# A hybrid attention layer on eight cores: the last tile's second MLP matmul by rows, and more filler held back where a buffer is waited for

## The reference

```python
proj = h @ w_in                       # 9728 columns: dilated q/k/v for 3 groups, q1,q2,k1,k2,v, two gates
y_a  = combine(dilated_attention(g) for g in 3 groups) @ w_proj_a     # windows of 128 keys, dilation 1, 4, 16
o_b  = (softmax(q1 k1) - lam * softmax(q2 k2)) @ v                    # causal over all 8192 keys, 8 heads
y_b  = (rms_norm(o_b) * (1 - lam_init)) @ w_proj_b
mix  = (sigmoid(gate_a) * y_a + sigmoid(gate_b) * y_b) @ w_out
h    = layer_norm(alpha * h + mix)
y    = layer_norm(alpha * h + square(relu(h @ w_mlp1)) @ w_mlp2)      # 1024 -> 4096 -> 1024
```

## Time and profile before

| | |
|---|---|
| runs | 4638.4, 4642.36 and 4921.69 us, median 4642.36 |
| the profiled execution | 4640.14 us; its span 4638.6 us, 1.5 us lie around it |
| slowest core / the other even cores | 4638.6 / 4621.7, 4619.8, 4614.2 us |
| odd cores | 4495.3 to 4510.2 us |
| PE busy on the slowest core | 4324.6 us, 93% |
| ACT, DVE, POOL busy | 2608.1, 1749.8, 854.4 us |

### The profile page before, as it was taken

How to read it: one execution, slowest core, us unless ns; L and a number is a source line. 1 busy time by engine, 2 the same in 40 slices (tenths; PEclk the granted TensorE clock), 3 DMA queues, 4 the chain that set the end, 5 groups by cost and what they waited for, 6 DMA issues and landing times.

```text
span 4638.6 us, 99445 instructions; the slowest of 8 cores (4495.3 to 4638.6 us)
## 1 busy us (share of the span) xinstructions
PE 4324.6 (93%) x37017; PEld 2471.5 (53%) x37400; DVE 1749.8 (38%) x3732; ACT 2608.1 (56%) x3329; POOL 854.4 (18%) x1113
## 2 busy tenths in 40 slices
PE   7898999799999899989988999999999999999998
PEld 3444454444455455445544655756657557566565
DVE  1655645412123322660033153242541533424353
ACT  1465655621166666677765566666665666767610
POOL 2000003311100011340013213022131130220322
PEclk9999999999999999999999999999999999999999
DMA  8665557877657866796476455474673664745363
GB/s 141 163 160 110 120 120 198 220 162 152 133 129 187 195 141 138 200 281 138 105 192 152 128 181 144 139 199 137 177 183 115 205 163 142 205 123 173 93 202 122
DMA packets 554463, 738.50 MB, mean 159 GB/s; under 512 B 165250, under 2 KB 352770, under 8 KB 552066
## 3 DMA queue, kind: packets, MB, share of 16 engines
q1 hardware_dynamic: 448450, 449.91, 35.7%
q0 software_dynamic: 105536, 282.11, 26.1%
HBM read 630.15 MB, written 191.87 MB: 177 GB/s over the span
## 4 chain that ended last, share of the span: by engine, by line
PE 79%; DVE 6%; DMA 5%; ACT 4%; issue 4%; SPq 2%; POOL 0%; DVEq 0%; ACTq 0%; POOLq 0%
PE PSB L639 48%; PE PSB L1388 19%; PE PSB L1360 11%; ACT m_PT_44 L425 1%; SPq L208 1%; DMA m_WR_147<-wp 1%; SPq L203 1%; DMA VA<-m_VAS_86 1%; DVE m_OO_50 L1431 1%; DVE m_TT_49 L1426 1%; DMA m_AK_97<-KA 1%; PE PSB L1489 1%; PE PSB L1523 1%; ACT m_PT_46 L425 1%; DVE m_TT_49 L1437 1%
## 5 line engine op out<-in xcount | busy, mean ns | idle before, releaser
L425 ACT ACTIVATE m_PT_43<-PSB 128x1024 bf16<-128x1024 f32 x544 | 556.8, 1023 | 577.1 <-PE PSB L1360 453.8
L425 ACT ACTIVATE m_PT_45<-PSB 128x1024 bf16<-128x1024 f32 (+1 forms) x544 | 530.2, 975 | 452.2 <-PE PSB L1360 371.4
L425 ACT ACTIVATE m_PT_44<-PSB 128x1024 bf16<-128x1024 f32 (+1 forms) x544 | 540.8, 994 | 0.1
L425 ACT ACTIVATE m_PT_46<-PSB 128x1024 bf16<-128x1024 f32 (+1 forms) x544 | 514.6, 946 | 2.1 <-DVE PSB L1372 1.7
L1372 DVE TENSOR_TENSOR PSB<-PSB,m_BT_72 128x512 f32<-128x512 f32 (+1 forms) x156 | 86.6, 590 | 196.5 <-PE PSB L1360 196.1
L1360 PE MATMUL PSB<-m_QB_69,m_KB_114 64*128 64x512 bf16 (+1 forms) x672 | 105.4, 378 | 31.3 <-DMA m_KB_114<-KTB 11.9
L1372 DVE TENSOR_TENSOR PSB<-PSB,m_BT_71 128x512 f32<-128x512 f32 (+1 forms) x156 | 86.2, 590 | 115.4 <-PE PSB L1360 115.3
L639 PE MATMUL PSB<-m_X1A,m_WR_146 128*128 128x512 bf16 x512 | 123.1, 379 | 1.7 <-ACT m_T_178 L425 1.0
L639 PE MATMUL PSB<-m_X1A,m_WR_149 128*128 128x512 bf16 x512 | 123.2, 379 | 1.3 <-DVE m_T_176 L1076 0.4
L639 PE MATMUL PSB<-m_X1A,m_WR_147 128*128 128x512 bf16 x512 | 122.4, 379 | 1.5 <-DVE m_T_178 L1076 1.0
L639 PE MATMUL PSB<-m_X1A,m_WR_148 128*128 128x512 bf16 x512 | 121.9, 379 | 1.3 <-ACT m_T_178 L425 0.9
(11 more groups left out here) (870 smaller groups left out, 10055.7 us busy)
## 6 DMA issues: line engine op xcount, KB each, us to landing
m_WR_146<-WB POOLq DMA_DIRECT2D x84, 512.0 KB, 6.3
m_WR_147<-WB POOLq DMA_DIRECT2D x84, 512.0 KB, 6.3
m_WR_148<-WB POOLq DMA_DIRECT2D x84, 512.0 KB, 6.0
m_WR_149<-WB POOLq DMA_DIRECT2D x84, 512.0 KB, 6.3
WB<-wm POOLq DMA_DIRECT2D x84, 256.0 KB, 20.4
m_VB_118<-VB SPq DMA_DIRECT2D x68, 258.0 KB, 4.8
m_VB_120<-VB SPq DMA_DIRECT2D x68, 258.0 KB, 4.6
m_KB_114<-KTB SPq DMA_DIRECT2D x68, 256.0 KB, 5.3
```

The source lines that it names most:

```text
L425: return self.P.op("scalar", lambda e: e.activation(out=out, in_=in_, func=func, bias=bias, scale=scale), 165.0 + 0.861 * n, rd, wr, gen)
```

## The change

The change has four parts.

1. In the last tile, `mlp2` runs block by block: the outer loop is s, the inner one q. The four W2 units of the quarters 2 and 3 have rooms of their own (`WZ`, which the order shows as `m_WZ_114` to `m_WZ_116` and `m_WZb_139`), laid over buffers of attention and gates that are no longer in use by then. They are loaded on POOL's queue at the start of the last tile's `mlp1`. The weight sequence of that tile ends with the four units of the quarters 0 and 1, which stay in the ring to the end.
2. The planner's estimate of when a DMA transpose has landed uses 130 bytes per ns in place of 300. Only the order follows from it; the DMA itself is the same.
3. `ensure` notes that it had to wait (`waited`), and `run` then fills for 8000 ns beyond the time of the unit's buffers, whether or not they are late; a first unit has no margin of its own any more, only the 1500 ns of any late unit.
4. `fill_until` may take 200 steps in place of 60.

```diff
-            done += slow / 60.0 + (nbytes - slow) / 300.0
+            done += slow / 60.0 + (nbytes - slow) / (130.0 if turn else 300.0)
...
-        self.soon = False
+        self.soon = self.waited = False
...
+        self.WZ = mk("WZ", [4096], BF16, 3, [a0])
...
+        self.WZ += mk("WZb", [4096], BF16, 1, [e2 - 8192])
...
-                w += [("m", M_W2 + i) for i in range(8)]
+                w += [("m", M_W2 + i) for i in range(4 if g[1] == self.tiles[-1] else 8)]
...
     def mlp1(self, t, wk):
...
+        if t == self.tiles[-1]:
+            for i, b in enumerate(self.WZ):
+                P.dma("gpsimd", b.ap, D["WB"][M_W2 + 4 + i], "g_" + b.name, 1 << 20, [self.dW[M_W2 + 4 + i]], gen=[b], split=2)
...
     def mlp2(self, t, wk):
...
+        rows = t == self.tiles[-1]
+        W = {}
+        for q, s in [(q, s) for s in range(4) for q in range(4)] if rows else [(q, s) for q in range(4) for s in range(4)]:
+            if q not in W:
+                W[q] = self.WZ[2 * q - 4:2 * q - 2] if rows and q > 1 else [self.weight(wk + 2 * q + i, "m", M_W2 + 2 * q + i) for i in range(2)]
...
+            if s == 3 and not rows:
+                self.release_w(2)
+                self.look_ahead(False)
...
         while L not in self.have:
+            self.waited = True
...
-        for _ in range(60):
+        for _ in range(200):
...
-            if t > P.T["tensor"]:
-                self.fill_until(t + (6000.0 if first else 1500.0))
+            self.fill_until(t + (8000.0 if self.waited else 1500.0 if t > P.T["tensor"] else 0.0))
+            self.waited = False
```

## The result

The changed kernel takes 4607.92 us (median of the first timing); the kernel before beside it 4642.36 us. The ratio is 0.9926, with a 95% interval from 0.9899 to 0.9952; timed a second time on another chip it was 0.9929 (0.9914 to 0.9945). For the sum of parts I use a second measure that scatters less than the slowest core, the mean span of the four even cores.

What follows compares the result with a forecast made beforehand. PE was taken as the bound, busy 4324.6 of 4638.6 us. From 4640.1, -7 - 3 - 9 + 1.5 + 0 - 5 + 0.3 + 1 = -21 gave 4619 profiled, median near 4620; whole range 4598 to 4646, the forecast's own 4610 to 4630.

Steps and rivals of the forecast that it cites:

- more is gained: Rival, chance 0.1: both O1 waits and the first wait go entirely, with their lost clock; -39 us, 4602.
- First unit: First QK matmul's 7.75 us wait for its K tile: 24 more filler matmuls fit in it; -7 us.
- Units held back: Wait of 4.20 us at 456.7 us: 12 more filler matmuls move ahead of it; -3 us.
- Filler dealt out differently: Between 400 and 2000 us: no wait seen to open or close; 0, with 8 us either way.
- Transposes: Second tile's O1: five bare units fill two waits, 19 us together, landing unchanged; -9 us.
- The bare units' bill: Units elsewhere that lose their filler: 0.3 to 0.5 us each where no wait covers it; +1.5 us.
- the waits move on: Rival, chance 0.2: at O1 the next K tile or the transpose comes later; total -8.5 us, 4632 to 4634.
- Last tile: Last tile by rows: -5 us behind PE's last matmul, +0.3 for a W2 wait, +1 for delayed W1 loading.
- slower: the new loads starve the ring: Rival, chance 0.1: in the last tile the fifth W1 unit lands late behind 4 MB; +4 us, 4644 to 4646.

Runs made afterwards that it cites:

- The smaller margin: Changed kernel with a margin of 4000 in place of 8000 for the first unit alone; 0.9944 of the kernel before.
- the eleventh buffer: Changed kernel with eleven staging buffers for the projections' output, not ten, and last-tile quarters in order 0, 2, 3, 1; 0.9916 of the kernel before.
- the whole filler part: The 8000 ns margin after a buffer wait and the 200 steps; alone, against the kernel before, 0.9951.
- the part alone: Kernel before with only the planner's cost of transposes changed, 130 in place of 300; 1.0014.

## Why the prediction was right in sign and wrong in its parts

The change is faster, as forecast, and the last tile's end and the first O1 of the second tile came by the mechanisms named. That the total lies in the range is in part luck: the first unit (7 us) and the transposes (7.5 us) gave little or nothing, and a term put at 0 gave about 20. The rival "more is gained" (4602) is near by its number and not by its mechanism, which was the whole of the two O1 waits and of the first one.

- **First unit, -7 forecast, none measured.** The step that failed is "24 more ... fit in the wait. The transfer doesn't depend on them." It looked at the K transfer alone. Three groups of filler need three staging buffers, the third was still full, and its store stood behind the loads the wait was for. The smaller margin and the eleventh buffer both showed it. The sign that was named for it, a first QK wait below 3 us, failed with 7.7 to 12.5 us.
- **Units held back, -3 forecast, -7 to -8 at that place.** The mechanism was right and the size was not: I counted 12 matmuls and the one wait of 4.20 us. By the order of weight loads on PE, the filler done ahead grows by 24 matmuls between 428 and 460 us (from 16 to 40), and short waits around that one close too.
- **Filler dealt out differently, 0 with 8 us either way.** This is the term that was mis-sized: 811 to 2383 us gives about -20 (-8, -2, -7, -5 by stage, against -1, 0, -3 and +1 in the old order). The wait at 1603 us on ACT, 3.8 us on core 0, is missing on every even core of the three kernels with the whole filler part that I compare, and stands on every even core of the kernel before and of the two parts without it (2.1 to 4.8 us). About 40 filler matmuls are done before that stretch there and not in it; that this is why was not tried by itself. For the dilated stage my statement "the filler between the units is the same in both orders. So that stays" was half right: PE's and SP's orders are the same there, and yet the waits for dilated keys fell from 16.3 to 6.0 us in the kernels with the filler part. Why those transfers come sooner against PE isn't settled; POOL and DVE do the same number of multiplications ahead of them in both.
- **Transposes, -9 and +1.5 forecast.** At O1 the five units fitted and the landing stayed put (28 to 33 us behind the first transpose's issue on the four even cores, 30 to 38 before): -6 to -9 in the kernels with this cost, against -3.5 to +1 without. The bare units' bill was under-sized where the part stands alone: +8 from 2511 to 4359 us, 4 to 6 of them at a weight that lands late and not the 0.3 to 0.5 us per unit. Beside the filler part it is 0 to +4, and kernels without the cost have +2 to +3 there. In sum the part alone costs 5 us by the mean, and beside the filler it is worth 2 us or nothing. The rival "the waits move on" was right that the gain is given back, and wrong in how: not at the next K tile or the transpose, but at a weight 1500 us later. The Trainium skill states that transposes run as fast as regular transfers ("Advanced Engine Details and Errata", section "X-Bar Transpose (TRN2)"). By it the O1 gain would have been nil; the runs disagree, 6 to 9 us, though none of them times a transpose beside a regular transfer of the same packets.
- **Last tile, -5 + 0.3 + 1.** The normalisation was right to 0.1 us (-4.9). The wait for the fourth W2 unit was 2.3, not 0.3: I took the issue time of the kernel before, and the change had moved squares so that POOL issued it 1.3 us later; and I counted its landing, 4.6 us, from the issue of the first of its two halves, where PE used it 5.7 us after that. The rooms cost PE nothing or up to 0.7.
- **The rival "slower: the new loads starve the ring"** fell clearly: the engines moved up to 435 GB/s with the deep queue, above the 339 from which I worked, and the fifth W1 unit was 1.7 us early.

## What to carry to other kernels

Filler that is put ahead of a late transfer must have everything it needs itself, its output buffers and their stores too; count them as well as the time. A loop limit in a planner can be what decides: with the old limit the larger margins changed nothing. Moving work early in a program pays where the work was crowded, which may be far from the wait it was moved for, so look at the crowded stretches and not only at the longest wait.

## What the runs showed of the hardware

- With fourteen loads of 512 KB issued within 8 us, the engines of one core moved 407 to 435 GB/s in half of the slices, above the 339 GB/s that I had scaled from a busy share. The Trainium skill ("DMA: Bandwidth & Descriptors", section "Where 436 GB/s comes from") puts the fabric's ceiling at about 435 and the memory's share of a core at about 358, and says that for loads from memory the latter binds; in this stretch the core moved more than that share.
- The same weight load of 1 MB reached its use 7.8 to 8.5 us after its issue in five kernels and 12.0 to 13.8 in another with the same order of matmuls around it, on all four even cores each. A term that rests on one such landing is uncertain by 4 us as long as what shares the queues with it is not known.
